# First norm's modulation columns on two engines, condition rows fetched by DMA, and the order around that norm's root

## What is computed

```python
cond_lat = jax.nn.silu(c)[:, None, :]
cond_ctx = jax.nn.silu(c_ctx)[None, None, :]
for i in range(DEPTH):
    mod_l = jnp.split(cond_lat @ ada_w[i] + ada_b[i], 6, axis=-1)
    mod_c = jnp.split(cond_ctx @ ada_w[i] + ada_b[i], 6, axis=-1)
    u = _modulate(_rms_norm(h, norm_mix[i]), mod_l[0], mod_l[1])
    uc = _modulate(_rms_norm(hc, norm_mix[i]), mod_c[0], mod_c[1])
    ...
    h = h + mod_l[5] * _sq_relu_mlp(_modulate(_rms_norm(h, norm_ffn[i]), mod_l[3], mod_l[4]), ffn_w1[i], ffn_w2[i])
```

## Time and profile before

| | us |
|---|---|
| median of 3 runs | 3567.66 |
| lowest, highest | 3564.20, 3570.67 |
| the profiled execution's own time | 3561.91 |
| its span in the profile | 3560.2 |
| TensorE busy (share) | 3242.3 (91%) |
| VectorE busy | 1881.3 (53%) |
| ScalarE busy | 1170.2 (33%) |

### The profile page before, as it was taken

One profiled execution on the slowest core, in us unless ns is written; L12 is line 12 of the kernel. 1 busy time (PEld: TensorE's weight loads), 2 busy tenths in 40 slices (PEclk: granted clock), 3 DMA queues, 4 the chain that ended last, 5 costly groups with the idle time before them and its releaser, 6 DMA issues.

```text
span 3560.2 us, 44175 instructions
## 1 busy us (share of the span) xinstructions
PE 3242.3 (91%) x18456; PEld 2699.3 (76%) x18456; DVE 1881.3 (53%) x2747; ACT 1170.2 (33%) x1757; POOL 208.9 (6%) x144
## 2 busy tenths in 40 slices
PE   8998889999989779999998999988998888997997
PEld 8877778888877667777777878756887777775776
DVE  2765646655434664777454342574434544456543
ACT  3315331212232554222342333253212534425322
POOL 0002100000010000000001220000001012000001
PEclk9999999999989999999999999999999799989997
DMA  4454113333212002555221123102122222310321
GB/s 177 136 180 146 45 48 126 123 130 119 95 54 70 3 1 95 177 177 177 95 93 70 64 71 113 42 1 80 54 72 89 76 68 86 112 58 9 100 87 59
DMA packets 90926, 318.73 MB, mean 90 GB/s; under 512 B 10006, under 2 KB 11926, under 8 KB 89960
## 3 DMA queue, kind: packets, MB, share of 16 engines
q1 hardware_dynamic: 81348, 288.91, 24.5%
q10 hardware_dynamic: 9380, 26.99, 2.1%
HBM read 294.12 MB, written 21.74 MB: 89 GB/s over the span
## 4 chain that ended last, share of the span: by engine, by line
PE 78%; DVE 10%; ACT 8%; issue 4%; DMA 0%; ACTq 0%; POOL 0%; POOLq 0%; DVEq 0%; SPq 0%
PE PS L384 77%; ACT whi L195 2%; ACT Pq L1246 1%; DVE STs L1283 1%; PE PS L387 1%; ACT nt L588 1%; DVE JUNK L491 1%; DVE stage L491 1%; DVE STq L1283 1%; ACT Ps L1246 1%; DVE wlo L209 1%; ACT U L593 0%; DVE fg L693 0%; ACT Ht L2276 0%; ACT FS L1637 0%
## 5 line engine op out<-in xcount | busy, mean ns | idle before, releaser
L384 PE MATMUL PS<-U,whi 128*128 128x512 f32 (+1 forms) x5408 | 1176.7, 363 | 89.3 <-DVE U L613 24.1
L384 PEld LDWEIGHTS PS<-U,whi 128*128 128x128 f32 x5408 | 912.3, 192 | 278.0 <-issue 54.1
L209 DVE TENSOR_TENSOR wlo<-stage,whi 128x1024 fp32r<-128x1024 f32 x339 | 417.6, 1233 | 1107.8 <-ACT whi L195 1107.2
L195 ACT ACTIVATE whi<-stage 128x1024 fp32r<-128x1024 f32 x339 | 358.4, 1058 | 1459.3 <-PE PS L384 1424.5
L384 PE MATMUL PS<-U,wlo 128*128 128x512 f32 (+1 forms) x2704 | 621.4, 356 | 0.0
L384 PE MATMUL PS<-Y,whi 128*128 128x512 f32 (+1 forms) x2240 | 581.7, 363 | 18.3 <-DVE Y L695 12.2
L384 PEld LDWEIGHTS PS<-U,wlo 128*128 128x128 f32 x2704 | 458.5, 190 | 80.0
L384 PEld LDWEIGHTS PS<-Y,whi 128*128 128x128 f32 x2240 | 396.5, 191 | 93.1 <-DVE Y L695 14.2
L384 PE MATMUL PS<-Y,wlo 128*128 128x512 f32 (+1 forms) x1120 | 367.2, 362 | 0.0
L384 PE MATMUL PS<-whi,U 128*128 128x512 f32 (+2 forms) x832 | 237.2, 374 | 11.3 <-DVE mV L1018 6.4
L384 PEld LDWEIGHTS PS<-Y,wlo 128*128 128x128 f32 x1120 | 208.6, 190 | 34.9
(11 more groups left out here) (408 smaller groups left out, 3329.3 us busy)
## 6 DMA issues: line engine op xcount, KB each, us to landing
stage<-in_w SPq DMA_DIRECT2D x128, 512.0 KB, 3.3
stage<-in_ada SPq DMA_DIRECT2D x80, 512.0 KB, 3.3
stage<-in_adb SPq DMA_DIRECT2D x48, 512.0 KB, 3.3
stage<-in_p_mg SPq DMA_DIRECT2D x16, 512.0 KB, 3.3
stage<-in_p_ma SPq DMA_DIRECT2D x16, 512.0 KB, 3.4
stage<-in_p_ms SPq DMA_DIRECT2D x16, 512.0 KB, 3.4
stage<-in_wo SPq DMA_DIRECT2D x16, 512.0 KB, 3.3
GS<-FS ACTq DMA_DIRECT2D x20, 384.0 KB
```

What stands on the lines that cost most here:

```text
L195: act.activation(self.parts[r % n][0], self.stage[i % len(self.stage)], ACT.Copy).then_inc(*self.S.up("w_hi", i))
L209: dve.tensor_tensor(lo, self.stage[i % len(self.stage)], hi.bitcast(F32), ALU.subtract).then_inc(*self.S.up("w_lo", i))
L384: return pe.matmul(o, l, r, start=start, stop=stop_, skip_group_check=True)
```

## The change

- The condition rows of a block (`crow`, latent and context) are laid out in DRAM and come to all 128 partitions by one DMA of 1 MB (`cond_rows`), instead of by matmuls and copies from PSUM. ScalarE takes a sigmoid, VectorE multiplies (`act_silu`, `dve_silu`). At the start this DMA is the first on ScalarE's queue; in each FFN it is issued by SyncE behind the wait for the norm's last lower part.
- The 16 first columns are shared: tiles 0 to 8 on VectorE from the transposed weight (`dve_first(t)`, 18 instructions, bias included), tiles 9 to 15 on TensorE (`pe_first(t)`), with VectorE adding their bias (`dve_first_rest`). The squares' sums stand between VectorE's tiles, and on TensorE the sums of the norm ahead of tile 14.
- `CB0` lies elsewhere, and ScalarE copies it to the old place (`CB3`) after the norm's last product (`act_move`).
- ScalarE rounds three weight tiles ahead of the root and the fourth behind the norm. VectorE makes the three lower parts behind the reciprocal, the fourth behind the norm.
- The order of the DMAs at the start is new, and ScalarE and VectorE no longer wait for CM before the condition's exponentials.

```diff
@@ place and making of the condition rows, the first columns @@
-        CB = [[place(f"CB{n}{v}", [128, 1024], F32, o + 4096 * v)[:, :] for v in range(2)]
-              for n, o in enumerate((offH + 12288, offZ + 16384, offZ + 16384))]
+        CBB = [place(f"CB{n}", [128, 2, 1024], F32, o)[:, :, :]
+               for n, o in enumerate((offY2 + 16384, offZ + 16384, offZ + 16384, offH + 12288))]
+        CB = [[c[:, v, :] for v in range(2)] for c in CBB]
...
+        def cond_rows(n):
+            return A["crow"][n // 2, :, :].partition_broadcast(128)
+
+        def act_silu(act, n):
+            for v in range(2):
+                if v:
+                    act.wait_ge(*at("cb", n, 0))
+                else:
+                    act.wait_ge(*at(f"cond_in{min(n, 1)}", n))
+                act.activation(JUNK, CB[n][v], ACT.Sigmoid).then_inc(*up("cb_sig", n, v))
+
+        def act_move(act):
+            act.wait_ge(*at("n_mul", 0, 7))
+            act.activation(CBB[3], CBB[0], ACT.Copy).then_inc(*up("cb_moved"))
+
+        def dve_silu(dve, n):
+            for v in range(2):
+                dve.wait_ge(*at("cb_sig", n, v))
+                dve.tensor_tensor(CB[n][v], CB[n][v], JUNK, ALU.mult).then_inc(*up("cb", n, v))
+
+        PE_FIRST = range(9, 16)
+
+        def pe_first(pe, t):
+            if t == 9:
+                s = B.take(pe, "first", ("mod", "first"))
+                pe.wait_ge(*at("first_in9"))
+            else:
+                s = B.of("first")
+                if t % 2 == 0:
+                    pe.wait_ge(*at(f"first_in{t // 2}"))
+            for k in range(8):
+                last = mm(pe, s[:, 2 * t:2 * t + 2], FIRST[t // 2][:, t % 2, 128 * k:128 * k + 128], SCs[:, 2 * k:2 * k + 2],
+                          t == 9 and k == 0, k == 7)
...
+        def dve_first(dve, t):
+            for v in range(2):
+                if t % 2 + v == 0:
+                    dve.wait_ge(*at(f"first_in{t // 2 if t < 8 else 8}"))
+                    dve.wait_ge(*at("cb", 0, 1))
+                if t and v == 0:
+                    dve.wait_ge(*at("mod", "row", t - 1, 0))
+                tile = FIRST[t // 2][:, t % 2, :]
+                dve.tensor_tensor_reduce(tile if v else JUNK, tile, CB[0][v], 1.0, col("ada_b0", t), ALU.mult, ALU.add,
+                                         MODS[0][:, 2 * t + v:2 * t + v + 1]).then_inc(*up("mod", "row", t, v))
@@ act_norm_mod, at its end; dve_norm_mod, behind dve_root @@
+            if r == 0:
+                W.hi(act, -1)
+                act_move(act)
...
+            if r == 0:
+                dve_lo(dve, -1, 3)
@@ pe_ffn, act_ffn, dve_ffn @@
-                    if g == 0 and k == 1:
-                        pe_spread(pe, L + 1, ("n_lo", 2 * L + 1, 7))
...
-                        act_spread(act, L + 1, ("n_lo", 2 * L + 1, 7))
+                        act_silu(act, L + 1)
...
+                    if n == 1:
+                        dve_silu(dve, L + 1)
@@ pe_program @@
-            pe_first(pe, 0)
-            pe_root_sums(pe, 0, squares(0), 6, ("n_mul", 0, 7))
-            pe_first(pe, 1)
+            pe.wait_ge(*at("cond", 3))
+            for t in PE_FIRST:
+                if t == 14:
+                    pe_root_sums(pe, 0, squares(0), 6, ("n_mul", 0, 7))
+                pe_first(pe, t)
             pe_root_spread(pe, 0, 6)
-            pe_spread(pe, 0, ("cond", 3))
@@ act_program @@
-            for g in range(0, 8, 2):
+            act.dma_start(CBB[0], cond_rows(0)).then_inc(*dma("cond_in0", 0))
+            for g in (0, 1, 6, 2, 3):
                 act.dma_start(FIRST[g][:, :, :], first_of(g)).then_inc(*dma(f"first_in{g}"))
+            act.dma_start(FIRST[4][:, 0, :], A["ada0"][8, :, :]).then_inc(*dma("first_in8"))
             act.wait_ge(*at("cl_in"))
-            act.wait_ge(*at("cm_in"))
...
+            act_silu(act, 0)
...
-            W.hi(act, -1)
+            W.hi(act, -1, 3)
@@ dve_program @@
-            dve_squares(dve, 0, TOK)
-            dve_lo(dve, -1)
-            dve_first(dve)
+            dve_silu(dve, 0)
+            dve_first(dve, 0)
+            dve_first(dve, 1)
+            dve_squares(dve, 0, TOK, range(1, 4))
+            dve_first(dve, 2)
+            dve_first(dve, 3)
+            dve_squares(dve, 0, TOK, range(4, 7))
+            for t in range(4, 9):
+                dve_first(dve, t)
+            dve_first_rest(dve)
@@ sp_program @@
-            for g in range(1, 8, 2):
-                sp.dma_start(FIRST[g][:, :, :], first_of(g)).then_inc(*dma(f"first_in{g}"))
+            sp.dma_start(FIRST[4][:, 1, :], A["adaf"][0, :, :]).then_inc(*dma("first_in9"))
+            sp.dma_start(FIRST[5][:, :, :], first_of(5)).then_inc(*dma("first_in5"))
+            for h in range(2):
+                sp.dma_start(HT[:, 4 * h:4 * h + 4, :], A["hT"][:, 4 * h:4 * h + 4, :]).then_inc(*dma(f"h_in{h}"))
+            sp.dma_start(FIRST[7][:, :, :], first_of(7)).then_inc(*dma("first_in7"))
...
+            W.load(sp, T("w1_0", 0) + 7)
+            sp.wait_ge(*at("n_lo", 1, 7))
+            sp.dma_start(CBB[1], cond_rows(1)).then_inc(*dma("cond_in1", 1))
```

More of the change, by code:

```diff
@@ L53 @@
     "rows_dve": ("m_vd", "g_vd", "s_v", "q_v"), "v_norm": ("v_st", "v_ag", "v_rr", "v_n", "v_n1", "v_n2"),
-    "qk_norm": ("q_rr", "q_nz"), "sigmoid": ("b_sig", "q_gs", "v_sig", "g_sig", "m_o"),
+    "qk_norm": ("q_rr", "q_nz"), "sigmoid": ("cb_sig", "cb_moved", "b_sig", "q_gs", "v_sig", "g_sig", "m_o"),
     "gated": ("q_g", "v_sg", "g_gate"), "rotated": ("r_sin", "r_cos"), "max_off": ("a_neg", "a_off"),
@@ L57 @@
     "m_head": ("m_h", "m_hn"), "m_div": ("m_den", "m_hrec"), "summed": ("sq_sum", "a_sum"),
[L58 to L61, removed]
+    "max_in0": ("first_in0", "m_din0"), "max_in1": ("first_in1", "m_din1"), "reach_in0": ("first_in6", "m_rin0"),
+    "reach_in1": ("first_in2", "m_rin1"), "spilled": ("first_in3", "spill", "m_spill"), "pool_m": ("m_band", "m_q"),
+    "in1": ("first_in9", "sgu_in1"), "in3": ("first_in5", "g_in_a2"), "in5": ("first_in7", "g_in_mk"),
+    "in7": ("cond_in1", "rot_in"), "part_in0": ("xs_in0", "gate_in0"), "part_in1": ("xs_in1", "gate_in1")}.items() for event in events}
 class Signals:
@@ L185, in load, with hi @@
             self.loaded += 1
-    def hi(self, act, used):
+    def hi(self, act, used, ahead=4):
         n = len(self.parts)
-        while self.rounded < min((self.part[used] if used >= 0 else -1) + n + 1, len(self.split)):
+        while self.rounded < min((self.part[used] if used >= 0 else -1) + ahead + 1, len(self.split)):
             r = self.rounded
@@ L196, in hi, with lo @@
             self.rounded += 1
-    def lo(self, dve, used, modulation):
+    def lo(self, dve, used, modulation, ahead=4):
         n = len(self.parts)
-        limit = (self.part[used] if used >= 0 else -1) + n
+        limit = (self.part[used] if used >= 0 else -1) + ahead
         while self.rest < len(self.plan):
@@ L441, in trunk_kernel @@
         JUNK = place("JUNK", [128, 1024], F32, offZ + 34848)[:, :]
-        def pe_spread(pe, n, ready):
+        def cond_rows(n):
+            return A["crow"][n // 2, :, :].partition_broadcast(128)
+        def act_silu(act, n):
             for v in range(2):
[L446 to L451, removed]
@@ L453, in act_spread @@
-        def act_spread(act, n, *free):
-            for v in range(2):
[L455 to L471, removed]
@@ L473, in dve_first @@
-        def dve_first(dve):
-            mods[0] = None
[L475 to L480, removed]
+                if v:
+                    act.wait_ge(*at("cb", n, 0))
+                else:
+                    act.wait_ge(*at(f"cond_in{min(n, 1)}", n))
@@ new lines, in act_silu @@
+                act.activation(JUNK, CB[n][v], ACT.Sigmoid).then_inc(*up("cb_sig", n, v))
[3 more added lines that the diff above has]
+        def dve_silu(dve, n):
+            for v in range(2):
+                dve.wait_ge(*at("cb_sig", n, v))
[12 more added lines that the diff above has]
+                          t == 9 and k == 0, k == 7)
+            if t == 15:
+                last.then_inc(*up("first"))
@@ L482, in dve_modulation, with dve_first_rest @@
+        def dve_first_rest(dve):
+            dve.wait_ge(*at("first"))
+            dve.tensor_tensor(MODS[0][:, 18:32].rearrange("p (t v) -> p t v", v=2),
+                              B.of("first")[:, 18:32].rearrange("p (t v) -> p t v", v=2),
+                              col("ada_b0", 9, 7).unsqueeze(2).to_broadcast([128, 7, 2]), ALU.add).then_inc(
+                                  *up("mod", "first"))
+            dve.wait_ge(*at("mod", "first"))
+            mods[0] = None
         def dve_modulation(dve):
@@ L484, in modulation @@
                 b, L = int(name[2] == "b"), int(name[-1])
-                n = 2 if b else L
+                n = 2 if b else (1 if L else 3)
                 for v in range(2):
                     m = 2 * t + v
-                    dve.wait_ge(*at("cb", n, v))
```

(17 more changed lines are left out.)

4 lines of the change are left out of this document (removed).

## The result

The changed kernel takes **3522.53 us** in the median of four runs (3518.86 to 3531.48), the kernel before 3565.93 beside it; the ratio is 0.9896, 95% interval 0.9865 to 0.9928. A later series of both kernels gave 0.9893 (0.9867 to 0.9919). The profiled execution took 3518.86 us, its span 3516.7 (3560.2 before).

A forecast was written before the change was run, and what follows sets the result against it. TensorE was taken to bound the kernel (78% of the wait chain), with data possibly bounding a shorter start. 24.9 us (start) plus 7.0 (FFNs), less 0.2, off the 3567.66 median gave 3536 us; range 3530 to 3545.

The forecast's parts named there:

- 1. *Data: Start, DMA queues: hT's halves land at 19.5 and 24.7 us, pair 6 at about 26.2, weight tiles at 32.5 to 37.5.
- 2. *Condition rows: Start: the 1 MB broadcast takes 6.3 us (bounds 5.4 and 10); sigmoids and products on ScalarE and VectorE end at 11.8.
- 3. *VectorE: Start: modulation tiles 0 to 8 at 1.205 us an instruction, between sums of squares, end at 44.3 us.
- 4. *TensorE: Start: tiles 9 to 15 and the sums of squares end at 45.0 us, within 1 us of VectorE.
- 5. *Root: Root spread ends at 49.0, three lower parts at 49.7; first U record at 55.1, first projection 24.9 us earlier.
- 6. *Behind the norm: After the start's norm: ScalarE's next rounding comes about 1 us late, covered by busy TensorE; 1 us if uncovered.
- 7. *FFNs: Each FFN loses 32 spread records, 3.49 us, 7.0 for both; 5.9 us of table, sigmoids and products stay hidden.
- 8. *The clock.: First projection tile, after the root: starts at TensorE's lower clock level, as after the first FFN's norm, at cost 0.
- The 1.4 us: First projection tile: 48 records wholly at the low clock, 15.2 us against 13.8; not taken into the sum.
- the sum: Whole kernel: 24.9 at the start plus 7.0 in the FFNs, less 0.2; median 3536 us, profiled span near 3528.5.
- My rivals: Data late 0.13, FFN cover gone 0.06, more than reckoned 0.10, clock low past first tile 0.02 plus 0.04, change does nothing 0.01.

## Why the prediction was right in its parts and wrong in the time

1. *Data*: right to 2.4 us. hT's halves feed ScalarE at 20.89 and 26.09 (19.5, 24.7 reckoned), pair 6 TensorE at 25.87 (26.2), three weight tiles land by 33.7, 36.2 and 39.9 (32.5, 35, 37.5). One figure was misreckoned: ScalarE's 1.13 MB in 10 us are 113 GB/s, not 104, which by the same sum puts pair 6 at 25.8.
2. *Condition rows*: landed in 5.5 us (6.3 taken, bounds 5.4 and 10), but the products end at 14.8, not 11.8. ScalarE issues its transfers first, the last until 7.24 us, and only then loads a table:

```profile
3.87 3.37 ACTq L2399 DMA_DIRECT2D first<-in_ada  x1
7.33 1.28 ACT L2347 ACT_TABLE_LOAD   x1 [7.33 <-issue]
```

   The 3 us lie in VectorE's idle, of which 2.6 are left.
3. *VectorE* ended its tiles at 45.4 (44.3), 4. *TensorE* at 45.56 (45.0), both by the hT landings.
5. *Root*: three lower parts 46.47 to 49.92 (46.0 to 49.7), past the spread's end at 49.5 by 0.4; first U record 55.19 (55.1); gain 24.8 (24.9). That this is right to 0.1 us has some luck in it: they began 0.5 late and took 3.45 us, not 3.73.
6. *Behind the norm*: hidden, the shift doesn't change there.
7. *FFNs*: 3.49 each as reckoned, no wait of TensorE at tile 5. Table and products are covered.
8. *The clock.* For the first projection tile it was right: low from 53.2 to 60.1 us, and the lead is 24.8 us ahead of it and 24.8 behind (92.84 against 68.05). The row:

```profile
53.30:60.00 6.70, 4.81 (x14) 4.13 (x15) 5.52 (x7) 6.70 (x12) 0.00 (x0) 0.50 0.06 25
```

   The 1.4 us that the prediction would have taken off by the Trainium skill (TensorE: Matmul & The Clock Gate, Part 1) didn't show.

**The step that failed is the sum**: "24.9 + 7.0 = 31.9 us, less 0.2 for the rest". "The rest" are some 3400 us of kernel in which TensorE's clock falls 43 times, taken as fixed. It isn't: up to `p_av` it gave back 3.4 us (31.8 to 28.35), in `p_av` it gained 13.3 (28.9 us at 1.2 GHz before, 15.1 at 2.4 after), behind it 1.9. The profiled span came out 11.8 below the 3528.5 of the sum, and that is -3.4 + 13.3 + 1.9. My rivals had the clock only as a loss and only at the start. The 3.4 and the 1.9 were not traced to their steps one by one. The range needed a term for it: a profile of the kernel before was at hand with a single long piece, 30.7 us at the lower level with TensorE without a gap, whose price either way is 13 us, and one run of the kernel before (3541.88), 22 us under the next, came only with the result.

## To carry over

Before you sum a change, list the long stretches at the lower clock in which TensorE has no gap. A shift of the code may turn one, as 1.7 us of matmuls did here, for nearly half its length (13.3 of 30.7 us), and the range must hold that. A gain that no step explains is to be looked for as a jump in the shift between two traces, not told as part of the change. And take a PSUM bank when its tile comes up: that was worth 22.6 us on the kernel before and 14.7 on the changed one in the median, where the waits that go add up to some 8. How much of the rest the pause ahead of `p_av` cost through the clock isn't shown.

## What the runs showed of the hardware

- The level can stay low under full load: TensorE was busy 28.90 of 28.90 us at 0.50 with 128-column records, in six profiles; in the ten others the same records ran at 1.00. The Trainium skill (TensorE: Matmul & The Clock Gate, Part 1) says that "the default state is throttled, and activity releases the throttle"; here being busy didn't.
- Work added can make a kernel faster: seven matmuls, 14 us in the median; seven more took it back.
- The place of a fall against the step before repeats to 0.2 us over launches and kernels, and a difference of 1.7 us turns it (97.4 low, 99.0 to 99.2 full, 100.7 to 100.8 low).
- The seventh transfer that ScalarE issued in a row held it for 3.37 us, where the first took 0.41 (2.93 to 3.39 in the other profiles of the changed start).
